# Attention unit of a two-block float32 transformer kernel: VectorE order inside the unit, and the order of the merge product

## The reference

```python
# per layer, for x (and in layer 0 also for the context stream xc)
p = h @ w_in[l]                                   # conv pair, q, k, v, gates
u = a * sigmoid(g)                                # a, g: first 1024 columns of p
u = dwconv1d(u, dw, dw_b)                         # 31 taps, 512 channels
y_conv = silu(layernorm(u, ln_g, ln_b)) @ w_conv_out
y_attn = merge_heads(attention(q, k, v, k_ctx, v_ctx, rpb)) @ w_na_out   # 8 heads of 64
x = x + g1 * ((sig(g_conv) * y_conv + sig(g_attn) * y_attn) @ w_out)
x = x + g2 * conv_ffn(modulate(rmsnorm(x)))
```

## Time and profile before

| | |
|---|---|
| median of three runs | 2559.01 us (2557.73 to 2561.95) |
| profiled execution, its time | 2556.15 us |
| profiled execution, its span | 2554.5 us |
| TensorE matmul busy | 2268.1 us, 89% of the span |
| VectorE busy | 1957.9 us, 77% |
| ScalarE busy | 1284.5 us, 50% |
| mean granted TensorE clock | 0.958 of full speed |

### The profile page before, as it was taken

One profiled execution on the slowest core, in us unless ns is written; L12 is line 12 of the kernel. 1 busy time (PEld: TensorE's weight loads), 2 busy tenths in 40 slices (PEclk: granted clock), 3 DMA queues, 4 the chain that ended last, 5 costly groups with the idle time before them and its releaser, 6 DMA issues.

```text
span 2554.5 us, 49963 instructions
## 1 busy us (share of the span) xinstructions
PE 2268.1 (89%) x18080; PEld 2214.9 (87%) x18080; DVE 1957.9 (77%) x3354; ACT 1284.5 (50%) x2029; POOL 120.3 (5%) x231
## 2 busy tenths in 40 slices
PE   3777699977878999988999999997999999977998
PEld 3766599977778999977999999996999999977998
DVE  7997787969867766896998677668776776787555
ACT  3345266343655655456565544445544544565443
POOL 0000000000000000000000000001000000000000
PEclk9898799989989999999999999998999999998999
DMA  6554555764555556443787487584677677553654
GB/s 255 196 166 137 186 177 178 243 229 154 165 177 195 181 171 192 158 135 116 233 276 242 151 289 252 161 288 135 208 274 230 200 272 239 178 184 106 196 169 136
DMA packets 150509, 500.19 MB, mean 196 GB/s; under 512 B 16480, under 2 KB 21600, under 8 KB 149088
## 3 DMA queue, kind: packets, MB, share of 16 engines
q1 hardware_dynamic: 113472, 375.06, 43.6%
q0 software_dynamic: 32544, 119.03, 15.4%
q10 hardware_dynamic: 4352, 4.20, 0.5%
HBM read 497.16 MB, written 1.05 MB: 195 GB/s over the span
## 4 chain that ended last, share of the span: by engine, by line
PE 61%; DVE 22%; ACT 6%; DMA 5%; issue 5%; POOL 0%; DVEq 0%; SPq 0%; POOLq 0%; ACTq 0%
PE bank_pair L1437 19%; PE bank_pair L1439 19%; PE bank_pair L1438 19%; DVE arena L1043 5%; DMA modraw<-in_w_mod 4%; DVE w_lo L877 4%; DVE modraw L890 2%; DVE x_res L890 1%; PE ps_t L1444 1%; ACT w_hi L495 1%; DVE arena L1002 1%; DVE small L1103 1%; DVE h_lo L1008 1%; DMA arena<-in_w_mod 1%; PE bank_pair L1554 1%
## 5 line engine op out<-in xcount | busy, mean ns | idle before, releaser
L877 DVE TENSOR_TENSOR w_lo<-raw,w_hi 128x1024 fp32r<-128x1024 f32 (+3 forms) x772 | 841.6, 1109 | 278.9 <-ACT w_hi L495 276.6
L1437 PE MATMUL bank_pair<-h_hi,w_hi 128*128 128x256 f32 x3344 | 959.1, 287 | 23.4 <-DVE w_lo L877 23.4
L495 ACT ACTIVATE w_hi<-raw 128x1024 fp32r<-128x1024 f32 (+3 forms) x772 | 737.6, 965 | 436.2 <-PE bank_pair L1439 321.2
L1438 PE MATMUL bank_pair<-h_lo,w_hi 128*128 128x256 f32 x3344 | 952.5, 285 | 0.0
L1439 PE MATMUL bank_pair<-h_hi,w_lo 128*128 128x256 f32 x3344 | 952.1, 285 | 0.0
L1437 PEld LDWEIGHTS bank_pair<-h_hi,w_hi 128*128 128x128 f32 x3344 | 648.1, 194 | 34.2 <-DVE w_lo L877 21.7
L1438 PEld LDWEIGHTS bank_pair<-h_lo,w_hi 128*128 128x128 f32 x3344 | 648.5, 194 | 0.2
L1439 PEld LDWEIGHTS bank_pair<-h_hi,w_lo 128*128 128x128 f32 x3344 | 648.1, 194 | 0.0
L1437 PE MATMUL bank_pair<-e_both,w_hi 128*128 128x256 f32 x1774 | 515.0, 290 | 86.8 <-DVE e_both L1391 29.0
L1438 PE MATMUL bank_pair<-e_both,w_hi 128*128 128x256 f32 x1774 | 510.8, 288 | 0.0
L1439 PE MATMUL bank_pair<-e_both,w_lo 128*128 128x256 f32 x1774 | 510.3, 288 | 0.0
(11 more groups left out here) (211 smaller groups left out, 2165.2 us busy)
## 6 DMA issues: line engine op xcount, KB each, us to landing
modraw<-in_w_mod POOLq DMA_DIRECT2D x224, 512.0 KB, 4.7
raw<-in_w_gu SPq DMA_DIRECT2D x176, 512.0 KB, 4.7
raw<-in_w_up SPq DMA_DIRECT2D x132, 512.0 KB, 4.8
raw<-in_w_gate SPq DMA_DIRECT2D x48, 512.0 KB, 4.5
raw<-in_w_dn SPq DMA_DIRECT2D x64, 384.0 KB, 3.7
raw<-in_w_dn SPq DMA_DIRECT2D x64, 320.0 KB, 2.9
raw<-in_w_down SPq DMA_DIRECT2D x48, 384.0 KB, 3.8
raw<-in_w_down SPq DMA_DIRECT2D x48, 320.0 KB, 3.1
```

The source lines that it names most:

```text
L495: nc.scalar.activation(w_hi[:, p, HALF * f:HALF * f + w], raw[:, p, HALF * f:HALF * f + w], ACT.Copy)\
L877: nc.vector.tensor_tensor(w_lo[:, p, at], raw[:, p, HALF * f:HALF * f + w], w_hi[:, p, at].bitcast(F32), ALU.subtract).then_inc(lo_ready, 1)
L1437: nc.tensor.matmul(out, l[0], r[0], start=start, stop=False)
L1438: nc.tensor.matmul(out, l[0], r[1], start=False, stop=False)
```

## The change

VectorE's unit is put into another order. The taps come in three pieces (2, then 4, then 4 or 5; 10 in units 0 and 1, 11 in units 2 to 5). The first lies ahead of the maximum, the second behind it, in the place that `split_lo(following)` had ahead of the reciprocal; the split and the third piece come behind the reciprocal. In units 6 and 7, which have no taps, the first split stays ahead of the reciprocal. The low part of an output is formed one unit later, ahead of the maximum (`head_lo(h - 3)`), the last three after the units. The layer norm's steps of units 6 and 7 come directly behind the reciprocal. TensorE gets two further waits ahead of the outputs of units 6 and 7, for VectorE's reads of the layer norm's sums in the same banks. The merge stage's first slab is made by a function of its own: the attention's chunks of both halves first, then the wait for `ln_lo`, then the convolution's.

```diff
-CONV_AT = np.cumsum([0] + [CONV_SLAB] * 6 + [8] + [3, 8] * 4 + [8]).tolist() + [CONV_K * CONV_C]
+CONV_AT = np.cumsum([0] + [CONV_SLAB] * 6 + [2, 4, 4] * 2 + [2, 4, 5] * 4).tolist()
...
+                def head_lo(k):
+                    c, t = k // 2, k % 2
+                    at = slice(P * t, P * (t + 1))
+                    dve.wait_ge(att_hi, a0 + k + 1)
+                    nc.vector.tensor_tensor(e_lo[:, CONV_C + c, at], ps_o[:, t, 0:P], e_hi[:, CONV_C + c, at].bitcast(F32),
+                                            ALU.subtract).then_inc(att_lo, 1)
+
+                for h in range(NA_H + 1):
...
-                        if 1 <= h < LN_AT:
-                            conv_piece(l, 2 * h + 5, i)
+                        if h < LN_AT:
+                            conv_piece(l, 3 * h + 6, i)
+                        if h >= 3:
+                            head_lo(h - 3)
...
-                    if h < LN_AT:
-
-                        conv_piece(l, 2 * h + 6, i)
-                    if h < NA_H:
                         at = (h // 2, h % 2, h // 2 == s.bodies - 1)
-                        split_lo(following(s, *at), 1)
+                        if h < LN_AT:
+                            conv_piece(l, 3 * h + 7, i)
+                        else:
+                            split_lo(following(s, *at), 1)
 
                         dve.wait_ge(att_exp, a0 + h + 1)
                         nc.vector.reciprocal(small[:, 6 + h % 2, 2:4], small[:, 6 + h % 2, 0:2]).then_inc(att_inv, 1)
-                        split_lo(after_next(s, *at), 0)
-                    if h >= 2:
-                        c, t = (h - 2) // 2, (h - 2) % 2
...
+                    if h < NA_H:
+                        if h < LN_AT:
+                            split_lo(following(s, *at), 1)
+                            conv_piece(l, 3 * h + 8, i)
+                        split_lo(after_next(s, *at), 0)
+                    if h == NA_H:
+                        head_lo(NA_H - 3)
...
+                for k in (NA_H - 2, NA_H - 1):
+                    head_lo(k)
...
-                if s.kind == "merge" and p == 0 and is_first:
-                    pe.wait_ge(ln_lo, s.e0 + 4)
...
+            def merge_first(s):
...
+                pe.wait_ge(lo_ready, 2 * s.g0 + 2)
+                pe.wait_ge(att_lo, NA_H * (s.e0 // 4 + 1))
+                for f in range(2):
+                    part(f, 4)
+                pe.wait_ge(ln_lo, s.e0 + 4)
+                for f in range(2):
+                    part(f, 0).then_inc(half_done, 1)
...
+                        if h == LN_AT:
+                            pe.wait_ge(ln_centred, 2 * i + 1)
+                        if h == LN_AT + 1:
+                            pe.wait_ge(ln_ms, i + 1)
```

More of the change, by code:

```diff
@@ L1084, in do_gate @@
                 a0, keys, width = NA_H * i, 256 if is_ctx else 512, CONV_C * P
-                for h in range(NA_H + 2):
+                def head_lo(k):
[5 more added lines that the diff above has]
+                for h in range(NA_H + 1):
                     if h < NA_H:
@@ L1520, in half @@
                         if is_first and p == 0 and f == 0:
-                            if s.kind == "merge" and k == 4:
-                                pe.wait_ge(att_lo, NA_H * (s.e0 // 4 + 1))
                             if s.kind == "out" and s.arg["kind"] == "a":
@@ L1563, in slab_after_norm, with part @@
                             ins.then_inc(half_done, 1)
+            def merge_first(s):
+                def part(f, first_k):
+                    for k in range(first_k, first_k + 4):
+                        c = HALF * f + P * k
+                        ins = mm3(pb[0][:, f, T * (k // 4):T * (k // 4 + 1)], (w_hi[:, 0, c:c + P], w_lo[:, 0, c:c + P]),
+                                  (e_hi[:, k, :], e_lo[:, k, :]), k % 4 == 0, k % 4 == 3)
+                    return ins
+                pe.wait_ge(lo_ready, 2 * s.g0 + 2)
[5 more added lines that the diff above has]
+                    part(f, 0).then_inc(half_done, 1)
             def do_slabs(s):
@@ L1571, in body @@
                             slab_after_norm(s)
+                        elif s.kind == "merge" and is_first and p == 0:
+                            merge_first(s)
                         else:
```

## The result

The changed kernel took 2542.86 us, the median of four runs (2540.94 to 2547.11), beside 2560.48 us for the kernel before, four runs (2557.73 to 2564.28). The ratio is 0.9932, with a 95% interval of 0.9914 to 0.9951: 17.4 us faster, 12.5 to 22.0. The forecast was 17.3 us. Run beside its variants later, it came to 0.9935 [0.9919, 0.995].

The account below looks back on a forecast made before the run. VectorE's unit, work and waits, was taken to set the pace. Terms 2.4 + 3.6 + 5.2 + 1.8 + 3.4 + 2.4 = 18.8, less 1.5 for the clock, gave 17.3 us: 2541.7 us, range 2535 to 2550.

Parts of the forecast that it names:

- What bounds the kernel: Gate stages: VectorE's unit, work and waits, sets the pace; it idles 23.8 us in 20 places ahead of low parts.
- Units 0 to 5: Units 0 to 5 of three stages: gains of 2.4 us (context), 3.6 (main of layer 0) and 5.2 (layer 1).
- The wait ahead of the reciprocal: VectorE's main-stage units: a new wait for the exponential, 0.5 us in 12 units, 3.1 us with latencies.
- Waits for the copied context scores go: Main-stage units: taps and low part cover ScalarE's copy, and ScalarE finishes its unit earlier, so VectorE's waits go.
- TensorE only just keeps pace in layer 1: Layer 1 units: TensorE waits 0.4 us, and its next scores may start at 12.28 us, after it finishes at 12.25.
- Tails: Units 6, 7 and layer norm: gains of 1.8 us (context), 3.4 (main of layer 0) and 2.4 (layer 1).
- The clock: TensorE behind unit 6's new wait: one clock fall booked in three stages, costing 1.5 us; range zero to 4.5.
- The merge order at nothing: Merge's first slab: TensorE is 2.9 us earlier, 5 at the low clock, but the sigmoids hide it; no gain.
- Carried through whole: Everything behind a gate stage depends on it in order, so the full 17.3 us comes off the execution.

Follow-up runs that it names:

- experiment with late low parts: Changed kernel with taps and reciprocal in their old places and the old merge order, low parts still one unit later: 2547.79 us, ratio 0.9953 to the kernel before.
- two experiments: Changed kernel with the old merge order: 2541.09 us, ratio 0.9931; kernel before with the new merge order alone: 2559.87 us, ratio 1.0005.
- two more: Changed kernel with three of four sigmoids moved into the merge stage: 2535.57 us, ratio 0.9901; the same with the old merge order: 2538.54 us, ratio 0.9918.
- filled kernels: Changed kernel with 36 matmuls on zeros ahead of the out stage: 2539.78 us; also with later bias load and dealt-out sigmoids: 2526.74 us.

## Why the prediction was right

**What bounds the kernel** (VectorE's unit, its idle time from the late reciprocal): shown. VectorE's busy time didn't change, the idle time went, and the reciprocal's move alone gave 3.7 of 3.9 us in layer 0's units and 5.1 of 5.6 in layer 1's.

**Units 0 to 5:** each term within 0.5 us, all a little low. The wait ahead of the reciprocal was 0.43 us in the unit shown; with the bias load moved it went altogether. "Waits for the copied context scores go" held, but only one of its two reasons carries it. The taps and the low part ahead of the maximum don't: in the experiment with late low parts three taps and a low part stand there, and the scores still come 1.36 us late. That ScalarE is through with its unit earlier does it, by the early reciprocal. One reading was loose: TensorE's output is not made at 1135.40 but begun there, and done by 1136.4, still 4.8 us ahead of its rounding.

**"TensorE only just keeps pace in layer 1"**: it did, with waits of 0.26 us.

**Tails:** the chain was right, its terms 0.5 us too good in both main stages. TensorE ended output 5 at 17.45 for 17.2, and the SiLU table came at 21.5 (1172.71) for 21.0. In the context stage the traces without a fall have 22.05 us from the maximum, so 22.3 with the 0.21 of the low part ahead of it (as 23.57 is the 23.78 of the table's stretch), for the 22.1 worked out. In layer 0 some 1 us of the 2.91 is a low clock that the kernel before had: behind a wait of 2.62 us at 706.62 (granted clock 0.50 up to 710.5) its last transposes and outputs took 5.89 us to the SiLU table, where layer 1 took 4.46. That was in the measured 30.03 which the forecast started from, but not seen as a term. Which part of the change earns the tails is open: neither the early reciprocal alone nor the late low parts alone gave layer 1's 1.84 us, only both together.

**The clock:** one fall of 1.5 us was booked for three stages. The profile of the changed kernel has it in the context tail, 1.5 us (23.57 for 22.06), four of the nine have it in layer 0, and layer 1's tail never showed it: nine falls in nine traces. In the context stage it was not the same wait with two outcomes. The four traces without a fall in the tail have it one step earlier, behind the wait ahead of the scores of 6, as here in the kernel with the later bias load (TensorE: these scores, transposes, output 4, scores of 7; granted clock 0.50 between 196 and 198 us):

```profile
193.88 0.70 PE L1636 MATMUL bank_pair<-arena 64*128 64x256 f32 x4 [2.30 <-ACT arena L625]
198.96 0.62 PE L1650 MATMUL ps_t<-tab,arena 128*128 128x128 f32 x4
...
204.42 0.66 PE L1682 MATMUL ps_o<-arena 128*64 128x128 f32 x8 [0.24 <-DVE arena L1130]
205.01 0.70 PE L1636 MATMUL bank_pair<-arena 64*128 64x256 f32 x4
```

Scores and half took 5.1 us there for 3.6, so TensorE came to output 4 late, waited 0.24 us for 1.75 and kept its clock. That earlier fall cost nothing: from the first maximum to that of unit 6 all nine traces have 57.8 to 57.9 us, as VectorE set the pace. Here a fall cost time only where TensorE was on the chain.

**The merge order at nothing:** right for the place I looked at, by two experiments, and the sigmoids are what hid it, by two more. It missed a cost further on. A TensorE that gets ahead idles longer at the next place where it must wait, and restarts at the low clock: 1.3 us in layer 1. All six traces with the new order and no filling matmuls have it (27.2 to 27.6 us from first gate product to first update); of the five with the old order three have 26.04 to 26.05 (behind waits of 1.9 to 2.1 us) and two 27.5 (behind 2.7 and 3.0). So the cost is not the new order's alone. That the filled kernels are back at 26.03, at a granted clock of 1.00 for 0.50, shows it to be the clock.

**Carried through whole:** not in one execution. Of the 16.98 us that the gate stages gained, the profiled pair shows 9.1 in the span: 0.7 was lost before the first gate stage began (142.04 for 141.33), 3.2 in the merge and out stages (1.1, 0.8 and 1.3), 1.1 between the context's out stage and the next gate stage, and 2.9 behind the last stage. In layer 0 these stretches vary from trace to trace by more than that (76.3 to 81.7 us from first gate product to last update in the context stage) with the modulation loads, for which VectorE waits 11.1 us in the shortest and 16.7 in the longest. Of the 2.9 us, 1.7 are a fall of the clock once more: behind one and the same wait for ScalarE (2.87 us at 1448.28 before, 2.88 at 1436.31 after) the granted clock is 1.00 in the kernel before and 0.57 in the changed one. Ten of the thirteen traces have that fall, with either order; the profile of before is one of three that don't. Something else stays open: from the last update of layer 1's out stage to the end it is 1311.2 to 1311.8 us in the five traces with the old merge order and 1312.0 to 1314.5 in the eight with the new one, though nothing was changed there. The ratio of the merge order alone leaves room for it (up to 3.8 us slower).

**What of the number was luck:** the units gained 0.9 us more than forecast, the tails with the fall 1.2 less, and the 1.3 us behind layer 1's merge weren't counted. The parts are off by up to 1.3 us and the measured interval goes from 12.5 to 22.0, so that 17.4 meets 17.3 to 0.1 us is luck; the table of terms is the better witness.

## What to carry to other kernels

When an engine waits in every round, find what it itself delivered late one step earlier, here a 0.1 us reciprocal behind 1.1 us of splitting, before moving the instruction that waits. A move of the waiting instruction alone only helps where other work stands between its new place and the next thing that comes by the same path. An engine made faster off the critical path shows what it's worth only when that path is cut too, and until then it may pay for its lead with a low clock after a longer wait.

## What the runs showed of the hardware

A stretch of the program came out at one of two lengths some 1.5 us apart (22.05 or 23.57 us, 27.1 or 28.6, 26.04 or 27.5), by whether TensorE worked behind its wait at a granted clock of 0.50 (1.2 GHz) or 1.00. The length of the wait alone doesn't decide it. The changed kernel itself, run twice, took 27.12 and 28.74 us behind the same wait of 2.42 us in layer 0; waits of 2.3 us ahead of scores in the context stage went either way too. A wait of 1.27 us in layer 1 was never followed by a fall, the one of 1.75 us in the context stage was in all five traces that have it, and one of 4.5 to 4.75 us ahead of the out stage in all five. The Trainium skill ("TensorE: Matmul & The Clock Gate", "HAM oscillation — how this bites in real kernels") has bursts of matmuls between waits for DMAs each start at the low clock. The waits of 4.5 to 4.75 us agree, the shorter ones only in part; and of the falls only those on the chain cost time, 1.3 to 1.7 us each.
